# Couples of projections, tiles kept in PSUM, heads turned on VectorE, output projections begun inside the softmax

## The reference

```python
def second_block(x, mem, ...):
    for l in range(DEPTH):                       # 2 layers
        x = x + head_group_mixer(rmsnorm(x, mix_norm[l]), w_in[l], sb_norm[l], ret_norm[l], w_out[l])
        x = x + memory_cross_attn(rmsnorm(x, xa_norm[l]), rmsnorm(mem, mem_norm[l]), xa_wq[l], xa_wkv[l], xa_wo[l])
        x = x + peer_ffn(rmsnorm(x, peer_norm[l]), peer_wq[l], peer_keys[l], peer_u[l], peer_v[l])
    return rmsnorm(x, final_norm)

def head_group_mixer(h, w_in, sb_norm, ret_norm, w_out):
    ...
    sb_o = stick_breaking(sb_q, sb_k, sb_v)                    # 8 heads of 64
    ret_o = retention(rotary(r_q), rotary(r_k), r_v)           # 4 heads of 128
    ret_o = merge_heads(head_groupnorm(ret_o, ret_norm)) * jax.nn.silu(r_g)
    return jnp.concatenate([sb_o, ret_o], axis=-1) @ w_out

def rotary(x):
    ...
    return jnp.concatenate([x1 * cos - x2 * sin, x1 * sin + x2 * cos], axis=-1)

def peer_ffn(h, w_pq, sub_keys, expert_u, expert_v):
    ...
    top_s, top_i = lax.top_k(scores, K)          # scores of 8 heads x 2 x 128 keys, K = 16
    cand_s = top_s[..., 0, :, None] + top_s[..., 1, None, :]
    best_s, best_pos = lax.top_k(cand_s, K)
    gate = jax.nn.softmax(best_s, axis=-1)       # weights of the chosen experts
    ...
```

## Time and profile before

| | us |
|---|---|
| median of 3 runs | 3617.31 (3616.02 to 3625.23) |
| profiled execution | 3620.47 |
| its span | 3618.7 |
| TensorE busy | 3559.0 (98%) |
| VectorE busy | 2606.5 (72%) |
| ScalarE busy | 1585.3 (44%) |
| GpSimd busy | 1028.0 (28%) |

### The profile page before, as it was taken

One profiled execution on the slowest core, in us unless ns is written; L12 is line 12 of the kernel. 1 busy time (PEld: TensorE's weight loads), 2 busy tenths in 40 slices (PEclk: granted clock), 3 DMA queues, 4 the chain that ended last, 5 costly groups with the idle time before them and its releaser, 6 DMA issues.

```text
span 3618.7 us, 65624 instructions
## 1 busy us (share of the span) xinstructions
PE 3559.0 (98%) x22742; PEld 3266.2 (90%) x22742; DVE 2606.5 (72%) x4691; ACT 1585.3 (44%) x2204; POOL 1028.0 (28%) x436
## 2 busy tenths in 40 slices
PE   9999999999999999999999999999999999999999
PEld 7888888888888879998999999888889999998887
DVE  7868787777874566645479676888743697668887
ACT  3223323223322355456555555444465555554443
POOL 0000000000000000045688777000267687881000
PEclk9999999999999999999999999999999999999999
DMA  7555544554543324663467666777745476667776
GB/s 254 187 168 164 168 134 146 168 186 146 174 157 101 104 71 145 197 215 117 148 188 234 222 220 227 247 249 254 244 148 159 146 240 215 220 226 240 253 252 211
DMA packets 203269, 682.64 MB, mean 189 GB/s; under 512 B 22497, under 2 KB 24673, under 8 KB 193889
## 3 DMA queue, kind: packets, MB, share of 16 engines
q1 hardware_dynamic: 174162, 570.31, 48.9%
q10 hardware_dynamic: 28944, 110.11, 8.7%
HBM read 643.63 MB, written 36.70 MB: 188 GB/s over the span
## 4 chain that ended last, share of the span: by engine, by line
PE 83%; DVE 9%; issue 2%; POOL 2%; DMA 2%; ACT 1%; SPq 0%; DVEq 0%; POOLq 0%; ACTq 0%
PE bank L606 25%; PE bank L607 25%; PE bank L608 25%; POOL low L567 2%; PE bank L1193 2%; DVE low L1765 1%; PE bank L820 1%; DVE best_p L2320 1%; DVE top_i L2320 1%; DMA acts_in<-acts_spill 1%; PE bank L798 1%; DVE best L2316 1%; DVE sums L2385 0%; DVE sums L2388 0%; DVE choice L2391 0%
## 5 line engine op out<-in xcount | busy, mean ns | idle before, releaser
L567 POOL TENSOR_TENSOR low<-raw,high 128x1024 fp32r<-128x1024 f32 x432 | 1027.8, 2385 | 2246.4 <-DVE low L1765 1920.2
L1277 ACT ACTIVATE high<-raw 128x1024 fp32r<-128x1024 f32 x1040 | 1092.0, 1056 | 1230.0 <-PE bank L608 870.7
L606 PE MATMUL bank<-h_lo,high 128*128 128x256 f32 (+1 forms) x4080 | 1250.2, 306 | 9.3 <-DVE h_lo L1842 3.2
L607 PE MATMUL bank<-h_hi,high 128*128 128x256 f32 (+1 forms) x4080 | 1246.0, 305 | 0.0
L608 PE MATMUL bank<-h_hi,low 128*128 128x256 f32 (+1 forms) x4080 | 1246.0, 305 | 0.0
L606 PEld LDWEIGHTS bank<-h_lo,high 128*128 128x128 f32 x4080 | 779.7, 191 | 45.0 <-issue 5.3
L607 PEld LDWEIGHTS bank<-h_hi,high 128*128 128x128 f32 x4080 | 779.7, 191 | 32.7 <-issue 0.7
L608 PEld LDWEIGHTS bank<-h_hi,low 128*128 128x128 f32 x4080 | 779.8, 191 | 32.1
L1765 DVE TENSOR_TENSOR low<-raw,high 128x1024 fp32r<-128x1024 f32 x612 | 732.3, 1218 | 30.8 <-ACT high L1277 29.5
L606 PE MATMUL bank<-low,weighed_hi 128*128 128x512 f32 x1024 | 390.5, 381 | 6.2 <-DVE weighed_lo L1765 6.2
L607 PE MATMUL bank<-high,weighed_hi 128*128 128x512 f32 x1024 | 389.5, 380 | 0.0
(11 more groups left out here) (337 smaller groups left out, 4607.8 us busy)
## 6 DMA issues: line engine op xcount, KB each, us to landing
raw<-in_experts SPq DMA_DIRECT2D x512, 512.0 KB, 3.4
raw<-in_w SPq DMA_DIRECT2D x176, 512.0 KB, 4.2
late_raw<-in_mod_late ACTq DMA_DIRECT2D x64, 1024.0 KB, 4.9
acts_spill<-acts_out ACTq DMA_DIRECT2D x128, 256.0 KB, 2.3
acts_in<-acts_spill SPq DMA_DIRECT2D x128, 256.0 KB, 3.6
raw<-in_w_in SPq DMA_DIRECT2D x56, 512.0 KB, 4.2
raw<-in_w SPq DMA_DIRECT2D x64, 384.0 KB, 3.2
raw<-in_w SPq DMA_DIRECT2D x64, 320.0 KB, 3.6
```

The source lines that it names most:

```text
L567: pool.tensor_tensor(low[:, col], raw[:, col], high[:, col].bitcast(f32), ALU.subtract)\
L606: pe.matmul(out, a[0], b[1], start=start, stop=False, **more)
L607: pe.matmul(out, a[0], b[0], start=False, stop=False, **more)
L1277: act.activation(high[:, slot * UNIT:(slot + 1) * UNIT], raw[:, slot * UNIT:(slot + 1) * UNIT], ACT.Copy)\
```

## The change

- *Begun projections.* `first_tiles` and `begun`: in both softmaxes TensorE does parts of the first two output units between the last heads (9 matmuls each in block 1, 6 in cross attention), into the score banks that are free by then; `out_tiles` finishes them, and `add_tile` and `add_gained` read those banks. In block 1 the wait for the evacuations stands ahead of the first flip, not ahead of the whole softmax, and VectorE's low part of one unit goes behind the third maximum.
- *Couples.* `project_couple`: the first two units after a norm run over tiles 0 to 6 each, and then both over tile 7. In `add_last` the weights' low parts go ahead of `lower_gained` for all outputs but the last.
- *Tiles in PSUM.* The eight scaled memory tiles and peer h tiles are written to parts of banks 6 and 7, two at a time, in place of SBUF; the first square of a norm goes to a PSUM bank, where it is gathered.
- *Turned heads.* r_q and r_k are turned as they leave PSUM, by four VectorE instructions a tile (two half products with the sine on swapped halves, one with the cosine, one add), with tables that hold the norm's scale and the sign. The turning matmuls and the twelve VectorE instructions behind them are gone. GpSimd's entry waits for the masks (`stick_in`).
- *Order.* Three units of memory keys come ahead of the stick's sums and the fourth behind the scores of retention. The Silus move behind the roots of the stick's norm. Weight roundings go among the memory tiles (`high_of` with `used_behind`). The gates are normalised after the first of the index sums, not after both.

```diff
-            def out_tiles(rhs, n, ready=None, gained=False):
+            def first_tiles(rhs, banks):
+                w, done = {}, {0: 0, 1: 0}
+                def part(o, n=KD):
+                    if o not in w:
+                        w[o] = take()
+                    tiles = range(done[o], min(done[o] + n, KD))
...
+            def project_couple(outs, rhs, ready):
+                w = [take() for _ in outs]
...
+                for n in range(len(outs)):
+                    tiles(n, range(KD - 1))
+                for n in range(len(outs)):
+                    tiles(n, (KD - 1,)).then_inc(unit_used, 1)
...
+                    if n == 2 and banks_free:
+                        pe.wait_ge(S["evacuated"], banks_free)
                     if 2 <= n < count + 2:
                         flip(n - 2)
+                    for o, tiles in begin.get(n - count, ()):
+                        begun(o, tiles)
...
-            pe.wait_ge(S["evacuated"], T["evacuated"].value())
+            pe.wait_ge(S["head_rooted"], 2)
+            begun = first_tiles(pair(ao_hi, ao_lo), first_out(len(items)))
             softmax_heads(items, score, 2,
-                          lambda h, o, kt: av[:, kt, h // 4 * HD:(h // 4 + 1) * HD], 1, 512)
-            out_tiles(pair(ao_hi, ao_lo), TOK)
+                          lambda h, o, kt: av[:, kt, h // 4 * HD:(h // 4 + 1) * HD], 1, 512,
+                          begun, {-1: [(0, 3)], 0: [(0, 3)], 1: [(1, 3)], 2: [(1, 3)]}, T["evacuated"].value())
+            out_tiles(pair(ao_hi, ao_lo), TOK, begun=begun)
...
-                for c in range(4):
-                    pe.matmul(ps[4 + c][:, :], mix_const("turn_ret"), r_qk[:, 2 * c:2 * c + 2, :], start=True, stop=True)\
-                        .then_inc(S["head_turned"], 1)
+                for c in range(3):
+                    memory_keys(c, 4 + c)
+
                 wait("z_copied", 4)
-                for c in range(4):
-                    memory_keys(c, c)
-
...
+                memory_keys(3, 7)
+                keys_kept(2)
                 memory_keys(4, 6)
...
-                    low_parts(units - (then is not None and o == KD - 1))
+                    if not gained or o == KD - 1:
+                        low_parts(units - (then is not None and o == KD - 1))
...
+                def turned_tile(c):
+                    bank, other = ps[c % 4], swapped[:, c % 2]
+                    wait("unit_used")
+                    for here, there in ((slice(0, 64), slice(64, P)), (slice(64, P), slice(0, 64))):
+                        mark(dve.tensor_tensor(by_halves(other[here, :]), unpaired(bank[there, 0:TOK]),
+                                               by_halves(inverse_sin[there, :]), ALU.mult))
+                    settle()
+                    mark(dve.tensor_tensor(unpaired(bank[:, 0:TOK]), unpaired(bank[:, 0:TOK]), by_halves(inverse_cos), ALU.mult))
+                    settle()
+                    dve.tensor_tensor(by_halves(r_qk[:, c, :]), unpaired(bank[:, 0:TOK]), by_halves(other), ALU.add)\
+                        .then_inc(S["evacuated"], 1)
...
-                for c in range(4):
-                    used(1)
-                    wait("evacuated")
-                    act.activation(r_g[:, c, :], r_g[:, c, :], ACT.Silu).then_inc(S["gate_ready"], 1)
-                act.preload_act_table_set("natural_log_exp_and_others")
+                T["evacuated"].next(20)
+                act.preload_act_table_set("natural_log_exp_and_others")
                 used(4)
-                T["evacuated"].next(20)
+                T["evacuated"].next(4)
+                gates_kept = T["evacuated"].value()
...
-                    for k in range(2 * c - 8, 2 * c - 6):
-                        dve.scalar_tensor_tensor(out=h2[:, k, :], in0=x2[:, k, :], scalar=layer_vecs[:, 32 + k:33 + k],
-                                                 in1=ps[7][:, 0:TOK], op0=ALU.mult, op1=ALU.mult).then_inc(S["scaled"], 1)
                     if c > 4:
                         tile_low(2 * c - 10)
                         tile_low(2 * c - 9)
+                        wait("tile_low", 2)
+                    for k in range(2 * c - 8, 2 * c - 6):
+                        dve.scalar_tensor_tensor(out=scaled_tile_of(k), in0=x2[:, k, :],
+                                                 scalar=layer_vecs[:, 32 + k:33 + k], in1=ps[7][:, 0:TOK],
+                                                 op0=ALU.mult, op1=ALU.mult).then_inc(S["scaled"], 1)
```

More of the change, by code:

```diff
@@ L760, in down_tiles, with out_tiles @@
                         tile(o)
-            def out_tiles(rhs, n, ready=None, gained=False):
+            def first_tiles(rhs, banks):
[4 more added lines that the diff above has]
+                    tiles = range(done[o], min(done[o] + n, KD))
+                    done[o] = tiles.stop
+                    for k in tiles:
+                        mm = paired3(banks[o][:, 0:TOK], [part[:, k * P:(k + 1) * P] for part in w[o]], rhs(k), k == 0,
+                                     k == KD - 1)
+                    return mm
+                return part
+            def out_tiles(rhs, n, ready=None, gained=False, begun=None):
                 for o in range(KD):
                     wait("residual_added")
+                    if begun and o < 2:
+                        begun(o).then_inc(unit_used, 1)
+                        continue
                     if gained and o >= 2:
@@ L1286, in _, with square, squares @@
             T["spread"].n = 2
-            def square(x, sq, k, cols):
-                act.activation(sq[:, k, cols], x[:, k, cols], ACT.Square).then_inc(S["squared"], 1)
-            def squares(x, sq, cols):
+            def square(x, sq, k, cols, first=None):
+                out = first if first is not None and k == 0 else sq[:, k, cols]
+                act.activation(out, x[:, k, cols], ACT.Square).then_inc(S["squared"], 1)
+            def squares(x, sq, cols, first=None):
                 for k in range(KD):
-                    square(x, sq, k, cols)
+                    square(x, sq, k, cols, first)
             def residual_squares(x, sq, cols, units, table=True, gained=None):
@@ L1756, in gather @@
                     settle()
-                    old, new = [sq[:, 0, cols] if part is None or k == end else part for end in (1, KD - 2)]
+                    old = sq[:, 0, cols] if part is None else part
+                    new = sq[:, 0, cols] if part is None or k == KD - 2 else part
                     mark(dve.tensor_tensor(new, old, sq[:, k, cols], ALU.add))
@@ L1843, in lower_gained, with add_last @@
                                          op0=ALU.mult, op1=ALU.subtract).then_inc(S["split"], 1)
-            def add_last(layer, sub, cols, streams, units, x=x1, sq=squares1, gained=None, then=None):
+            def add_last(layer, sub, cols, streams, units, x=x1, sq=squares1, gained=None, then=None, first=ps[4:6]):
                 for o in range(KD):
@@ L1851, in add_last @@
                     wait("unit_used", units)
-                    add_tile(o % 2, o, layer, sub, streams, x)
+                    add_tile(o % 2, o, layer, sub, streams, x, first if o < 2 else ps[4:6])
+                    if gained and o < KD - 1:
+                        low_parts(units)
                     if gained:
@@ L1906, in add_gained, with softmax_heads @@
                 own_residual(KD)
[L1908 removed]
+            def softmax_heads(count, scale, keys, parts, n_out, low_behind=None):
                 def top_of(n):
@@ L2115, in _ @@
             settle()
-            low_parts(1)
             T["unit_used"].next(12)
             softmax_heads(16, lambda n: head_inverse[:, 8 + n:9 + n], 512, lambda n: [part[:, n // 2:n // 2 + 1, n % 2 * P:(n % 2 + 1) * P]
-                                                          for part in (ao_hi, ao_lo)], 1)
+                                                          for part in (ao_hi, ao_lo)], 1, low_behind=2)
             T["evacuated"].next(14)
             T["head_summed"].next(2)
-            add_last(1, 1, LAT, one, 1, then=(1, 2))
+            add_last(1, 1, LAT, one, 1, then=(1, 2), first=first_out(16))
             own_residual(KD)
@@ L2552, in constant_columns @@
     }
-    for name, half in (("turn_axial", 32), ("turn_ret", 64)):
-        turn = np.zeros((P, P))
-        for c in range(P):
-            if c // half % 2 == 0:
-                turn[c + half, c] = -1
-            else:
-                turn[c - half, c] = 1
-        one[name] = turn
+    half, turn = 32, np.zeros((P, P))
+    for c in range(P):
+        if c // half % 2 == 0:
+            turn[c + half, c] = -1
+        else:
+            turn[c - half, c] = 1
+    one["turn_axial"] = turn
     f = np.float32
```

142 lines of the change are left out of this document (81 added, 61 removed).

## The result

| | before | after |
|---|---|---|
| median of 4 runs each, us | 3621.27 (3616.02 to 3625.93) | 3586.77 (3585.72 to 3588.21) |
| profiled execution, its span | 3620.47, 3618.7 | 3586.45, 3584.7 |
| TensorE busy | 3559.0 | 3542.2 |

The changed kernel takes 0.9905 of the time before (95% interval 0.9888 to 0.9923), 34.5 us less by the medians and 34.0 by the two spans. The forecast was 3583 within 3574 to 3603. The total hides two errors, a loss of some 5 us and a gain of some 3 us, that cancel in part, and the loss showed how to make the kernel faster still.

A forecast was written before the change was run, and what follows sets the result against it. TensorE, busy 98% of the span, was taken as the bound, its idle time as the reserve. Terms summing to 36.0 us gave 3584.5 from the profiled execution, 3581.3 by the median; forecast 3583, range 3574 to 3603.

The forecast's parts named there:

- Attention and cross attention: Softmaxes: output matmuls fill TensorE's waits; 4.6 us saved in block 1, 4.85 in cross attention over both layers.
- add_last: Start of layer 0: low parts made first and a couple of units remove TensorE's waits; 4.8 us saved once.
- Turned heads, Silus: Both layers: z wait, turning matmuls and stick wait leave TensorE's path, less a stall in stick sums; 9.5 us saved.
- the new stall: Stick sums, each layer: TensorE waits 1.4 us for the first argument, 2 with semaphores and restart; bounds 0 to 3.5.
- Peer tiles: Peer queries: h tiles read from PSUM end the p_q_lo wait, 2 x 2.0 us, plus 3.4 of clock; 7.4 saved.
- the turning term: Turning matmuls removed from TensorE: 5.29 us in layer 0, 3.70 in layer 1, of which 0.3 overlaps the next group.
- Gates normalised first: VectorE's chain before the choice: same instructions in another order, 0 us; bounds -0.7 (a loss) to +1.5.
- The first rival: Clock: half-speed stretches follow the new stick-sums stall and the peer one stays; 6.8 us comes back, 3590; chance 0.18.
- signs of being wrong: Turned tiles above 2.6 us, a larger choice wait, half-speed stretches at new places, value products later than before.
- The third rival: Choice: TensorE arrives earlier but VectorE's selection does not, so the wait grows by up to 7.4 us; 3590; chance 0.13.
- The fourth: Rival: GpSimd let in earlier runs beside the stick's masks and delays TensorE some 2 us a layer; 3587; chance 0.09.
- The second rival: Turned tiles locked out by GpSimd's low parts take 7.6 us each, 29 us a layer; slower, 3641; chance 0.06.

The follow-up runs named there:

- gates_alone: The kernel before with only the gates normalised ahead of the second index sums; 3621.78 us, ratio 1.0011.
- peer_in_sbuf: The changed kernel with the eight peer h tiles in SBUF again, in the changed order of VectorE's instructions; 3594.28 us, ratio 0.9931.
- gates_and_key: The changed kernel with the gates' sums in PSUM and the fourth memory-key unit between the fourth and fifth stick sums; 3575.75 us, ratio 0.9877.
- none_begun: The changed kernel without begun projections in both softmaxes; 3597.58 us, ratio 0.9937.

## Why the prediction was right, and where it was not

*What bounds the kernel.* Right. TensorE's idle time was the reserve, and the terms read from its waits came out with an error of 0.7 or less in each of the first seven stretches of the table above: the working by rows, idle time plus restart, carries that far.

*Attention and cross attention.* Right, 4.8 and 4.4 for 4.6 and 4.85, and right for the reason given: the third output of cross attention now waits 0.8 (the waits on issue are that) and takes 0.95 of the gain back, as was worked out from the table load and the rounding. The 4.85 itself is a slip: the prediction's own terms, 3.2 less 0.95, make 2.25 a layer and not 2.4, and 2.2 was measured.

*add_last.* The size was right (5.0 for 4.8). The expectation for the run without couples put 0.75 of it to the couple, which is worth 0.2.

*Turned heads, Silus.* 8.8 for 9.5. The turned tile (1.8) came out as worked and the new stall (1.68) a little smaller than the 2 that was taken off. One term was wrong: the 0.65 a layer for the scores of retention waiting for the stick. That wait stands unchanged, 1.3 in both layers, because nothing was put between the last sum and these scores. The Silus alone are worth 1.2 a layer in the new order, not 1.7.

*Peer tiles.* 7.6 for 7.4 in the comparison of before and after; taken away alone they are worth 6.4, because the changed order of VectorE's instructions saves 1.2 in layer 1 without them.

*Luck in two terms.* 3.4 of the peer term and 1.6 of the turning term (5.29 against 3.70 in the earlier trace rows) are half-speed stretches of the one execution that was read. gates_alone has the same waits in layer 0, 1.5 for z and 1.9 for p_q_lo, and there the turns take 3.70 and the stretch behind p_q_lo has a clock of 1.00; its half speed came in layer 1:

```profile
1656.38 3.70 PE L1045 MATMUL bank<-r_qk,tables_m 128*128 128x512 f32 x8
...
1845.50:1852.40 6.90, 6.90 (x62) 6.90 (x63) 6.86 (x31) 4.29 (x7) 3.57 (x2) 1.00 0.49 152
...
2867.00:2874.00 7.00, 6.79 (x46) 6.79 (x47) 6.96 (x30) 3.02 (x5) 3.24 (x2) 0.76 0.48 153
```

So these 5 us fit so well because the forecast was read from the execution that it was then compared with; another execution of the same code can lose less, or lose it elsewhere.

*Gates normalised first: the step that failed.* "The same instructions stand on the same serial VectorE chain", with bounds of -0.7 to +1.5. The instructions are the same and their duration is not: this multiply of two SBUF tiles lasts until the GpSimd instruction beside it has ended, and at the new place it started with that instruction (a low part of 2.38), at the old one 0.86 before its end. Its 1.15 in the trace of before should have been read against the 0.42 of a tile with a PSUM operand: what is over 0.42 is a wait, and beside low parts of 2.38 it can grow to some 2.4 (an estimate from these two rows), 1.6 or so more a layer, so that the bound of -0.7 was too narrow. The wait for choice grew by 1.23 and 1.25, and the clock behind it gave up another 1.3 and 1.6: 5.4.

*The clock.* The first rival named the right mechanism at the wrong place: no half-speed stretch followed the stick's stall, in this trace or in the nine others that have it, and one followed the choice in both layers. A larger wait for choice and half speed at a new place were two of the signs of being wrong that the prediction had named. The third rival forecast a larger wait for choice, for another reason (TensorE earlier than VectorE); gates_alone shows that reason to be wrong, and peer_in_sbuf too. The fourth had GpSimd come in earlier, which it did; the masks beside it are covered by two units of keys now, so nothing was lost.

*The 3.4 at the output matmuls* were in no step. In the kernel before a half-speed stretch stood behind the first wait for weighed_lo in both layers, in the changed one in layer 0 alone, and of the later waits for weighed_lo two of 0.3 and 0.4 are gone and one of 1.5 is 1.0. The runs above show such a stretch come and go with the same wait in front of it (18 of 26 times, last section), so this gain is best taken as luck; that the change caused it is not shown.

*The second rival* (slower) is answered: from PSUM no turned tile waited for GpSimd, and with two SBUF inputs in its last instruction it still kept pace.

## What to carry to other kernels

When an instruction is moved, compare its duration with that of the same shape without company; the part above is a wait on whatever ran beside it, and it will be another one at the new place. Where VectorE and GpSimd work side by side, give one input of each two-input VectorE instruction to PSUM before reordering anything: here one line won 7.9 us by the medians and 7.0 at the choice by matmul starts, more than the reordering that it mended had cost (5.4). One SBUF input may be enough, though: ahead of the index sums, in both kernels, a shift with one input takes 2.47, a little more than a low part, and the mask of the same shape behind it 0.28. Whether GpSimd is the cause no run here tests. The two rows of the changed kernel:

```profile
L2446 DVE TENSOR_SCALAR half_u<-best_p x2: 2461/2466/2471, 1908.4 to 2917.1; 128x256 uint32<-128x256 uint32 x2
L2447 DVE TENSOR_SCALAR half_u<-best_p x2: 282/282/283, 1910.8 to 2919.5; 128x256 uint32<-128x256 uint32 x2
```

And check a total by the start times of the same matmul in two traces: errors that cancel, and the start of the program, are seen at once.

## Not expected of the hardware

- Behind the same wait of 2.0 (weighed_lo) the granted clock fell in layer 0 alone in the changed kernel and in layer 1 alone in gates_and_key. Behind waits of some 1.5 it fell once in the traces of before and after, behind z in layer 0 of the kernel before, and stayed at 1.00 behind z in layer 1, the choice of the kernel before and the stick's sums of the changed one. A half-speed stretch is a chance, worth 1.3 to 3.4 us here, and not a fixed price. Over the 14 traces it stood behind 13 of the 18 waits of 2.7 for choice, behind 18 of the 26 waits of 2.0 for weighed_lo, and behind 2 of the 42 waits of 1.4 to 1.6 for z, choice, the stick's sums or h_lo at the start of layer 1; it stood behind none of the 6 waits of 0.6 to 0.7 for choice.
- The first 45 us of the program vary by up to 5 us between executions of kernels that are equal there (the same matmul, about the 200th, starts between 54.0 and 59.0). The granted clock of that stretch, in the changed kernel and in none_begun:

```profile
24.00:44.00 20.00, 19.67 (x91) 14.93 (x89) 17.89 (x32) 8.79 (x14) 0.00 (x0) 0.83 0.96 365
```

```profile
24.00:44.00 20.00, 20.00 (x82) 15.54 (x81) 15.00 (x29) 6.70 (x10) 0.00 (x0) 0.75 0.97 367
```

  That alone is most of the difference between the totals and the sums by matmul starts above.
